# Attention values of a hybrid decoder step: 4-byte f32 products replaced by three fp32r products of split halves, from the second prompt tile on

## The reference, cut to what matters

```python
def _sparse_attend(q, k_sel, v_sel, valid):
    b, t = q.shape[:2]
    qg = q.reshape(b, t, N_KV_HEADS, N_HEADS // N_KV_HEADS, HEAD_DIM).astype(jnp.float32)
    logits = jnp.einsum('btkgd,btnkd->btkgn', qg, k_sel.astype(jnp.float32)) * (HEAD_DIM ** -0.5)
    logits = jnp.where(valid[:, :, None, None, :], logits, NEG_INF)
    p = jax.nn.softmax(logits, axis=-1)
    o = jnp.einsum('btkgn,btnkd->btkgd', p, v_sel.astype(jnp.float32))
    return o.reshape(b, t, ATT_DIM).astype(q.dtype)
...
    branch_b = attend(q, qi, wi, k, v, ki) * jax.nn.silu(z_b)
    merged = jax.nn.sigmoid(g_a) * (branch_a @ w_pa) + jax.nn.sigmoid(g_b) * (branch_b @ w_pb)
    y = x + gate * (merged @ w_out)
```

## Time and profile before

| | us |
|---|---|
| median of 3 runs (lowest, highest) | 3234.39 (3234.24, 3235.6) |
| profiled execution | 3241.45 |
| its span, first to last instruction | 3239.6 |

### The profile page before, as it was taken

How to read it: one execution, slowest core, us unless ns; L and a number is a source line. 1 busy time by engine, 2 the same in 40 slices (tenths; PEclk the granted TensorE clock), 3 DMA queues, 4 the chain that set the end, 5 groups by cost and what they waited for, 6 DMA issues and landing times.

```text
span 3239.6 us, 48142 instructions
## 1 busy us (share of the span) xinstructions
PE 3157.4 (97%) x18999; PEld 2748.9 (85%) x18999; DVE 1877.8 (58%) x3640; ACT 1101.5 (34%) x1960; POOL 836.9 (26%) x765
## 2 busy tenths in 40 slices
PE   7999999989999999999999999999999999999999
PEld 6999999957887888888887888889888788889987
DVE  5443695044535993035257999056436899947652
ACT  3444332345324221154244121154226312135431
POOL 2345675444510332012200331100310133010011
PEclk9999999999999999999999999999999999999999
DMA  8765688675864555622744556600563455650017
GB/s 296 253 213 196 225 277 283 243 254 162 297 229 157 207 192 203 233 92 81 257 158 151 195 195 213 229 30 11 201 216 118 156 195 198 222 184 11 9 39 237
DMA packets 262353, 592.52 MB, mean 183 GB/s; under 512 B 17485, under 2 KB 174343, under 8 KB 212466
## 3 DMA queue, kind: packets, MB, share of 16 engines
q1 hardware_dynamic: 251620, 551.57, 50.1%
q0 software_dynamic: 10368, 37.75, 3.5%
q10 hardware_dynamic: 142, 0.13, 0.0%
HBM read 448.93 MB, written 140.47 MB: 182 GB/s over the span
## 4 chain that ended last, share of the span: by engine, by line
PE 91%; DVE 3%; ACT 2%; DMA 1%; POOL 1%; issue 1%; another core or an unknown queue 0%; ACTq 0%; SPq 0%; DVEq 0%; POOLq 0%
PE ps L1171 84%; PE ps L1176 7%; DVE RS L1849 1%; DMA WR<-in_w_proj_b 1%; DMA GB<-gb_scratch 0%; DVE XN L1770 0%; POOL BBL L2446 0%; ACT SC L923 0%; DVE LP L2111 0%; POOL WLH L2285 0%; DVE OB L2122 0%; DMA WR<-in_w_in 0%; DMA ST<-in_state_conv 0%; DVE sKPT L2035 0%
## 5 line engine op out<-in xcount | busy, mean ns | idle before, releaser
L1171 PE MATMUL ps<-HTH,WLH 128*128 128x512 f32 x3504 | 1129.1, 391 | 0.0
L1171 PEld LDWEIGHTS ps<-HTH,WLH 128*128 128x128 f32 x3504 | 658.2, 188 | 139.2 <-issue 5.0
L1171 PE MATMUL ps<-HTL,WLH 128*128 128x512 f32 x1752 | 682.7, 390 | 0.0
L1982 DVE TENSOR_SCALAR_CACHE_REDUCE JUNK<-SC,SMALL 128x384 bf16<-128x384 f32 (+13 forms) x392 | 580.0, 1480 | 15.6 <-POOL sSC L2371 1.6
L1171 PE MATMUL ps<-H,WLH 128*128 128x288 f32 x3504 | 484.3, 299 | 4.7 <-DVE H L1809 2.0
L1171 PEld LDWEIGHTS ps<-H,WLH 128*128 128x128 f32 x3504 | 474.8, 191 | 6.6 <-issue 2.4
L1171 PEld LDWEIGHTS ps<-HTL,WLH 128*128 128x128 f32 x1752 | 329.3, 188 | 64.9
L2111 DVE CUSTOM_DVE_ANT_0 LP<-ps,SC,RQ 128x512 f32<-128x512 f32 (+3 forms) x320 | 201.8, 667 | 293.5 <-ACT SC L923 278.0
L887 ACT ACTIVATE T<-ps 128x512 f32<-128x512 f32 x192 | 114.7, 597 | 701.9 <-PE ps L1171 698.6
L2285 POOL TENSOR_TENSOR WLH<-WR,WLH 128x1024 fp32r<-128x1024 f32 x97 | 235.2, 2424 | 321.9 <-ACT WLH L710 321.8
L1171 PE MATMUL ps<-V,T 128*128 128x128 f32 x2016 | 264.1, 277 | 0.7 <-ACT T L1039 0.7
(11 more groups left out here) (344 smaller groups left out, 4536.6 us busy)
## 6 DMA issues: line engine op xcount, KB each, us to landing
WLH<-w_scratch SPq DMA_DIRECT2D x291, 1024.0 KB, 4.8
w_scratch<-WLH SPq DMA_DIRECT2D x97, 1024.0 KB, 5.8
WR<-in_w_in SPq DMA_DIRECT2D x73, 512.0 KB, 4.4
MW<-in_w_mod SPq DMA_DIRECT2D x6, 2048.0 KB, 16.2
q_scratch<-QO SPq DMA_DIRECT2D x32, 256.0 KB, 5.6
ma_scratch<-T SPq DMA_DIRECT2D x32, 256.0 KB, 5.6
gb_scratch<-GB SPq DMA_DIRECT2D x32, 256.0 KB, 5.9
QU<-q_scratch SPq DMA_DIRECT2D x64, 128.0 KB
```

Of the source, the lines that this page charges most:

```text
L1171: return pe.matmul(out, lhsT, rhs, start=start, stop=stop, **more)
L1982: ins_ = dve.tensor_scalar(JUNK[0:n, 0:row.shape[1]], row, MID[0:n, c:c + 1], 0.0, ALU.is_ge, ALU.add, accum_out=CNT[0:n, c:c + 1])
```

## The change

From tile 1 on, V and the transposed exponentials P are kept as high and low fp32r halves. V's high half is VR; its low half VLO goes to a DRAM scratch (`store_vl`) and comes back before attention into two of the three weight slots (`load_vl`, VL). POOL makes both halves of a new tile's values (`value_halves`) at the start of PROJ_B, and those of tile 0 in its wo stage (`first_value_halves`).

A group's values are now: `high_values` (VR with the high half PTH, VL with PTH), and a group later `low_values` (VR with the low half PTL). V stands still and P moves, 256 columns (both heads) at a time, so the output comes out transposed. `turn_p` runs two groups ahead. ACT makes PTH of all groups; DVE makes PTL from PSUM and PTH, each time; only in the eight units with `late_runs` POOL makes it for groups 1, 2, 4 and 5, for which ACT first copies the unrounded values too (PTW), since POOL doesn't read PSUM. `lengths` replaces `turn_out`: two products of ones with diagonals DG of 1/sum (made by POOL, `diagonals`) put 1/sum in the other half of the bank, and `finish` multiplies by both. `scale` is gone. Two of pb's first weights (one in tile 1) are loaded when the last value product is done instead of before attention. Some semaphores are merged, with no effect on the order.

```diff
-    on_act = lambda t, u, c: c < (LATE_COPIES if late_runs(t, u) else ACT_COPIES)
+    low_on_pool = lambda t, u, c: c in (1, 2, 4, 5) and len(late_runs(t, u)) > 0
+    p_low = lambda t, u, c: (p_low_pool if low_on_pool(t, u, c) else p_low_dve).at(t, u, c)
+    p_read = lambda t, u, c: (p_raw if low_on_pool(t, u, c) else p_low_dve).at(t, u, c) if t else p_copy_a.at(t, u, c)
...
+                if t and h >= 0 and BLOCKS * (t + 1) > 8 * h:
+                    load_vl(t, h)
+                elif j + 3 not in AFTER_PAGES:
                     load_w(j + 3)
...
+                sp.wait_ge(*pv.at(t, len(UNITS) - 1))
+                for h in range(2):
+                    if BLOCKS * (t + 1) > 8 * h:
+                        load_w(first + len(PROJ_A) + len(PROJ_B) + 1 + h)
...
+            act.activation((PTH if t else PT[t])[slot][:, 0:m], src, ACT.Copy).then_inc(*p_copy_a.mark(t, u, c))
+            if t and low_on_pool(t, u, c):
+                act.activation(PTW[slot][:, 0:m], src, ACT.Copy).then_inc(*p_raw.mark(t, u, c))
...
             for kk in range(min(2, n - 2 * c)):
                 k = 2 * c + kk
...
+                cols = slice(2 * kk * P, 2 * (kk + 1) * P)
+                mm(ps[acc][:, 0:256], VR[:, k, head], PTH[slot][:, cols], k == 0, False, skip_group_check=True)
+                mm(ps[acc][:, 0:256], VL[t][k // 8][:, k % 8, head], PTH[slot][:, cols], False, False, skip_group_check=True)
...
+            turn_p(t, u, 1)
             for c in range(groups):
-                if c + 1 < groups:
-                    turn_p(t, u, c + 1)
-                group_values(t, u, c)
+                if c + 2 < groups:
+                    turn_p(t, u, c + 2)
+                if c:
+                    low_values(t, u, c - 1)
+                if last and c == groups - 1:
+                    lengths(t, u)
+                high_values(t, u, c)
+            low_values(t, u, groups - 1)
...
+                    if t and u and hh and x == len(runs) - 1:
+
+                        probabilities_low(t, u - 1, 0)
...
+                groups = unit_groups(t, u)
+                for c in (1, 2):
+                    probabilities_low(t, u, c)
                 unit_sum(t, u)
                 if u:
                     finish(t, u - 1)
...
+                for c in range(3, groups):
+                    probabilities_low(t, u, c)
                 for b, r in late_runs(t, u):
                     choose(t, scores(t)[:, b, 0:width(BLOCKS * t + b)], P, b, b, r)
-                scale(t, u)
...
+        def diagonals(t, u):
+            pool.wait_ge(*scaled.at(t, u))
+            if u:
+                pool.wait_ge(*turned.at(t, u - 1))
+            pool.tensor_tensor(DG[:, :, :], ident[:, :].unsqueeze(1).to_broadcast([P, 4, P]),
+                               R4[u % 2].unsqueeze(2).to_broadcast([P, 4, P]), ALU.mult).then_inc(*diag.mark(t, u))
```

More of the change, by code:

```diff
@@ L1566, in group_values, with high_values @@
             acc = acc_bank(t, u)
-            pe.wait_ge(*p_copied(t, u, c))
+            pe.wait_ge(*p_copy_a.at(t, u, c))
+            if c == 0:
+                claim(acc)
+            head = slice((pr // 2) * HD, (pr // 2 + 1) * HD)
+            for kk in range(min(2, n - 2 * c)):
+                k = 2 * c + kk
+                for hh in range(2):
+                    ins_ = mm(ps[acc][:, hh * HD:(hh + 1) * HD], PT[t][p_slot(t, u, c)][:, (2 * kk + hh) * P:(2 * kk + hh + 1) * P],
+                              V[:, k, head], k == 0 and hh == 0, k == n - 1, skip_group_check=True)
+            ins_.then_inc(*pv.mark(t, u, c))
+            pv.values[t, u] = pv.n
+        def high_values(t, u, c):
+            blk, pr = UNITS[u]
+            n = BLOCKS * t + blk + 1
+            acc, slot = acc_bank(t, u), p_slot(t, u, c)
+            head = slice((pr // 2) * HD, (pr // 2 + 1) * HD)
+            pe.wait_ge(*p_copy_a.at(t, u, c))
             if c == 0:
@@ L1584, in head_values, with lengths @@
                 turn_p(t, u, 0)
+            turn_p(t, u, 1)
             for c in range(groups):
-                if c + 1 < groups:
-                    turn_p(t, u, c + 1)
-                group_values(t, u, c)
+                if c + 2 < groups:
[6 more added lines that the diff above has]
+            low_values(t, u, groups - 1)
+            if last:
+                freed[acc_bank(t, u)] = attn_z.at(t, UNITS[u])
+        def lengths(t, u):
+            acc = acc_bank(t, u)
+            pe.wait_ge(*diag.at(t, u))
+            for part_ in range(2):
+                ins_ = mm(ps[acc][:, 256:512], ones[:, :].bitcast(F32R), DG[:, 2 * part_:2 * part_ + 2, :].rearrange("p h q -> p (h q)"),
+                          part_ == 0, part_ == 1, skip_group_check=True)
+            ins_.then_inc(*turned.mark(t, u))
+            freed[acc] = attn_z.at(t, UNITS[u])
         def turn_out(t, u):
@@ L2398, in convolve, with value_halves, first_value_halves, probabilities_low @@
                 pool.tensor_tensor(x[0], x[0], x[4], ALU.mult).then_inc(*conv.mark(t, f, p))
+        def value_halves(t, f):
+            pool.wait_ge(*a_done.at(t, PROJ_A.index(("v", f)), "P"))
+            four = lambda ap: ap.rearrange("p (b d) -> p b d", b=BLOCKS)
+            place = VR[:, BLOCKS * t:BLOCKS * (t + 1), f * HD:(f + 1) * HD]
+            link(pool.tensor_copy(place, four(VO[f][:, :])))
+            pool.tensor_tensor(four(VLO[f][:, :]), four(VO[f][:, :]), place.bitcast(F32), ALU.subtract).then_inc(*v_low.mark(t, f))
+        def first_value_halves(f):
+            if f == 0:
+                pool.wait_ge(*pv.at(0, len(UNITS) - 1))
+                pool.wait_ge(*v_out.at(0, 1))
+                pool.wait_ge(*merged.at(0, KC - 1, "P"))
+            two = lambda ap: ap.rearrange("p (b d) -> p b d", b=2)
+            whole, high = V[:, 2 * f:2 * f + 2, :], two(VH0[f][:, :])
+            link(pool.tensor_copy(high, whole))
+            link(pool.tensor_tensor(two(VLO0[f][:, :]), whole, high.bitcast(F32), ALU.subtract))
+            pool.tensor_copy(VR[:, 2 * f:2 * f + 2, :], high.bitcast(F32)).then_inc(*v_low.mark(0, f))
+        def diagonals(t, u):
[4 more added lines that the diff above has]
+                               R4[u % 2].unsqueeze(2).to_broadcast([P, 4, P]), ALU.mult).then_inc(*diag.mark(t, u))
+        def probabilities_low(t, u, c):
+            if not low_on_pool(t, u, c):
+                return
+            m = 256 * min(2, BLOCKS * t + UNITS[u][0] + 1 - 2 * c)
+            slot = p_slot(t, u, c)
+            pool.wait_ge(*p_raw.at(t, u, c))
+            pool.tensor_tensor(PTL[slot][:, 0:m], PTW[slot][:, 0:m], PTH[slot][:, 0:m].bitcast(F32), ALU.subtract
+                               ).then_inc(*p_low_pool.mark(t, u, c))
         def branch_low(f):
+            if t and f == 2:
+                pool.wait_ge(*vl_out.at(t, 1))
+                pool.wait_ge(*v_out.at(t, 1))
             if t == 0 and f == KC - 2:
@@ L2475, in _ @@
                     gather_index_keys(i // 2 + 2)
+                if t and i == 0:
+                    value_halves(t, 0)
+                    value_halves(t, 1)
                 if i == (SAMPLE_ITEMS + 3 if t == 0 else 1):
@@ L2499, in _ @@
                         query_low(t, u + 2)
+                    for c in range(unit_groups(t, u)):
+                        probabilities_low(t, u, c)
+                    diagonals(t, u)
                     if u == len(UNITS) - 2 and t + 1 < TILES:
```

134 lines of the change are left out of this document (95 added, 39 removed).

## The result

| | before | after |
|---|---|---|
| median (lowest, highest), us | 3233.48 (3229.15, 3235.6) | 3243.47 (3240.76, 3247.11) |
| profiled execution | 3241.45 | 3240.76 |
| attention to pb, tile 1, tile 2, tile 3 | 118.6, 184.1, 247.5 | 118.3, 172.3, 268.6 |

What follows compares the result with a forecast made beforehand. PE's own back-to-back work was taken to bound attention. The terms -45 + 13 + 30 + 0 = -2 took the plain median of 3234.4 to 3232.4 us, range 3202 to 3256.

Steps and rivals of the forecast that it cites:

- Step 1: PE's value products in attention: 0.094 us less per key block, 504 blocks, less small extra costs: -45 us.
- rival C: PE in attention: each switch from transposes to fp32r products costs 0.08 us, 22 us in all; total 3245, chance 0.07.
- Step 2: Units without a late run: PE waits for low halves because of DVE's order, 0.85 us with n = 7 and 8; +13 us.
- Step 3: Tile 3's eight late units: `choose` behind the last low half delays masked pieces, and meets POOL; +30 us (23 to 41).
- Step 4: Tile edges: output turn, pb's late weight load, POOL's value halves and VL traffic; 0 us expected in sum.
- B: Late units: POOL meets `choose` in full, up to three times a unit, +41 instead of +30; total 3250, chance 0.20.
- mark of 17.5: Late units of tile 3: the period in us above which the rival of full POOL and `choose` meetings decides.
- A: Attention: the waits for DVE hide, wholly or in part; total 3200 or 3212, chance 0.24.
- D: PE's value products are no cheaper, as stationary V is reloaded for every 256 columns; gain nil, chance 0.03.

Runs made afterwards that it cites:

- first repeat: The changed kernel executed and profiled once more with no edit: 3234.48 us.
- split marking: The changed kernel with the first three operations of `choose` moved between DVE's low halves of groups 3 and 6 in late units: 3226.65 us, ratio 0.9981.

## Why the prediction was wrong

**Step 1 (-45) held.** Value products start 0.118 apart, `lengths` of units with n = 16 15.02 instead of 16.62. That is 1.60 less, where 16 x 0.094 = 1.50 was worked out and rival C's 0.08 in each of eight groups would have left 0.9: the change of form costs nothing. With the marking away from them, tile 3's late units too take PE's time as worked out (13.31 to 13.53 for n = 14, 13.3 forecast).

**Step 2 (+13) held**: the low product of group 3 is some 0.8 us late in tile 1's units with n = 7 and 0.6 with n = 8, tile 2 11.8 us shorter where -15.8 + 4.6 = -11.2 was worked out. The reordering of DVE removed the wait in tile 1, and made others.

**Step 3 (+30) is the step that failed, by a term that it lacked.** For the eight late units it said +30 - 8 x 13.5 x 0.094 = +19.8 against before. Measured: the periods +26.8, and 3.9 more up to the first `lengths`, +30.7. With PE kept busy in the waits it is +20.0 and 2.4, 22.4. So 8.3 of the 10.9 us missing are the clock: an idle time of 2.5 us was priced at 2.5 us, but the work behind it may run at half speed, for up to 1.7 us more. The first repeat, with one fall and no extra products, says the same: its periods sum to 122.2, +21.4, and 2.4 before them, so +23.8. The other 2.6 are 0.3 a unit (17.24 to 17.85 instead of 17.1 with n = 14), with `choose` beside POOL at 5.1 to 5.5 us instead of 4.2 + 0.85. The prediction read the granted clock, 1.00, in stretches in which PE hardly waits, and carried it over to units in which it was itself forecasting waits.

**Step 4 (0) was low by some 2.5 us**, what is left when steps 1 and 2 are taken as worked out (+11.4 measured, -2 forecast, 10.9 in step 3). Of it 0.6 us three times is pb at half clock (45.2 for 44.6); PE's wait for POOL's BBL ahead of pb also grew, from 0.35 to 2.0 us, beside the turn that is gone. PE waited for no weight there.

**The rivals.** B's price (3250) was closer than the forecast, but by luck: its mechanism, up to three full meetings of POOL and `choose` a unit, came in part only. With n = 14 the diagonals met the first operation, 0.9 us, and QLOW cost up to 0.5; with n = 13 POOL's last low half and the diagonals met the first two (0.93 to 1.02 and 1.28 to 1.41 us long), and `choose` took 1.3 to 1.6 us more than before. What lifted the periods to 18 and 19 us, over its mark of 17.5, was the clock: without falls five of the seven stay below it and the last two are 17.60 and 17.85. The Trainium skill's rule ("SBUF — State Buffer", "Who interferes with whom") holds for single operations here: the subtraction of 128x2 with both inputs in SBUF took 1.28 us and ended with POOL's first low half, begun before it; the low halves from PSUM kept their 0.69. A fell: the waits don't hide. D fell with step 1. In sum, without the falls in the late units the change would stand at 3235.25, 1.8 us above before and within the noise, where -2 was forecast.

## What to carry to other kernels

When PE is the bound and a change makes it wait, look at the granted clock behind the waits, in more than one execution, and price it, or give PE something to do there. And when the bounding engine gets cheaper, work that was parked on its neighbours (here `choose` on DVE, and its relief on POOL) has to be placed anew: leaving the marking to the late units gained some 4 us before the change and cost 33 after it.

## What was not expected of the hardware

- The clock can fall to half for 3.4 us after PE waits of 1.84 to 2.9 us (and 4.8), in the split marking even where none was over 1.18, while one wait of 2.1 us and one of 2.7 never brought it down in four executions. With the same order and the same waits it fell in one, three, six and six of the late units of four executions. This alone moves tile 3 by 8 us.
- A fall cost 1.35 us in the late units, and 0.6 at the start of pb, where a full-speed PE waits for POOL.
- A DVE operation on 128x2 values took 1.28 us beside a POOL subtraction, and 0.16 us without one.
